# Splitting a third product of each pair once more, coupled over neighbouring couples, with two operands streamed from HBM

## What is computed

```
h    = rmsnorm(x, norm_g)
proj = einsum('btd,dc->btc', h, w_in)            # 1088 x 2048 x 10240
xa, za, v, bg, cg, zb, ga, gb = split(proj)
ya   = pool_mixer(xa, ...) * silu(za)            # trailing means, small 256x256 maps
yb   = bg * depthwise_conv3(cg * v) * silu(zb)
merged = sigmoid(ga + b) * (ya @ w_proj_pool) + sigmoid(gb + b) * (yb @ w_proj_conv)
y    = rmsnorm(x + merged @ w_out, final_norm_g)
```

## Time and profile before

| | |
|---|---|
| median of 3 runs | 2416.88 us |
| span of the profiled execution, first to last instruction | 2415.0 us |
| outside the span (run less span) | about 1.9 us |
| TensorE (PE) busy | 2392.6 us, 99% |
| VectorE (DVE) busy | 1700.3 us, 70% |
| ScalarE (ACT) busy | 894.0 us, 37% |
| GpSimd (POOL) busy | 116.0 us, 5% |
| granted TensorE clock | 0.998 of full speed over the span |
| HBM read and written | 172 GB/s over the span |

### The profile page before, as it was taken

How to read it: one execution, slowest core, us unless ns; L and a number is a source line. 1 busy time by engine, 2 the same in 40 slices (tenths; PEclk the granted TensorE clock), 3 DMA queues, 4 the chain that set the end, 5 groups by cost and what they waited for, 6 DMA issues and landing times.

```text
span 2415.0 us, 42738 instructions
## 1 busy us (share of the span) xinstructions
PE 2392.6 (99%) x17842; PEld 2332.7 (97%) x17842; DVE 1700.3 (70%) x2329; ACT 894.0 (37%) x1316; POOL 116.0 (5%) x220
## 2 busy tenths in 40 slices
PE   8999999999999999999999999999999999999998
PEld 7999999999999999999999999999999999888886
DVE  6676666666666586777868777765755887877676
ACT  7333333333333343323322222233533533532535
POOL 3010000000000000000000000000000011100000
PEclk9999999999999999999999999999999999999999
DMA  7563333232323454434433343345645767898656
GB/s 268 198 205 110 107 106 111 99 118 90 127 90 127 163 188 151 150 136 151 150 132 113 136 138 135 107 154 208 227 168 171 275 241 278 296 343 306 243 178 227
DMA packets 196655, 418.06 MB, mean 173 GB/s; under 512 B 12617, under 2 KB 114045, under 8 KB 182448
## 3 DMA queue, kind: packets, MB, share of 16 engines
q1 hardware_dynamic: 170928, 284.85, 35.0%
q0 software_dynamic: 23744, 125.24, 13.7%
q10 hardware_dynamic: 1792, 5.24, 0.6%
HBM read 281.00 MB, written 133.77 MB: 172 GB/s over the span
## 4 chain that ended last, share of the span: by engine, by line
PE 97%; DVE 0%; issue 0%; ACT 0%; DVEq 0%; POOL 0%; POOLq 0%; ACTq 0%
PE ps L1328 76%; PE ps L1475 12%; PE ps L1390 7%; PE ps L1497 1%; PE ps L1543 1%; DVE ops L2195 0%; ACT ops L1683 0%; DVE out L2458 0%; PE ps L1520 0%; DVE out L2511 0%; DVEq L226 0%; DVE h0raw L2612 0%; POOL rstd L1309 0%; ACT squares L1804 0%; ACT squares L1813 0%
## 5 line engine op out<-in xcount | busy, mean ns | idle before, releaser
L1328 PE MATMUL ps<-ops,hi 128*128 128x272 f32 x9728 | 1325.2, 288 | 0.1
L1328 PEld LDWEIGHTS ps<-ops,hi 128*128 128x128 f32 x9728 | 1264.5, 188 | 0.4 <-DVE ops L2195 0.3
L1328 PE MATMUL ps<-ops,lo 128*128 128x272 f32 x4864 | 708.6, 288 | 0.0
L1328 PEld LDWEIGHTS ps<-ops,lo 128*128 128x128 f32 x4864 | 647.4, 188 | 0.0
L1604 ACT ACTIVATE hi<-sb 128x512 fp32r<-128x512 f32 x440 | 278.2, 632 | 576.3 <-PE ps L1328 444.1
L2169 DVE TENSOR_TENSOR pb<-pb,ps 128x544 f32<-128x544 f32 x330 | 237.5, 720 | 261.8 <-PE ps L1328 261.6
L2025 DVE TENSOR_TENSOR lo<-sb,hi 128x512 fp32r<-128x512 f32 x440 | 303.1, 689 | 153.3 <-ACT hi L1604 148.7
L1604 ACT ACTIVATE hi<-raw 128x512 fp32r<-128x512 f32 x264 | 166.8, 632 | 371.6 <-PE ps L1328 357.6
L2025 DVE TENSOR_TENSOR lo<-raw,hi 128x512 fp32r<-128x512 f32 x264 | 181.8, 689 | 103.0 <-ACT hi L1604 103.0
L1475 PE MATMUL ps<-ms_hi,mt 128*128 128x512 f32 x896 | 221.3, 389 | 0.0
L1475 PEld LDWEIGHTS ps<-ms_hi,mt 128*128 128x128 f32 x896 | 168.2, 188 | 34.8
(11 more groups left out here) (173 smaller groups left out, 1580.2 us busy)
## 6 DMA issues: line engine op xcount, KB each, us to landing
raw<-in_w_in_dram SPq DMA_DIRECT2D x156, 512.0 KB, 4.0
pb<-part SPq DMA_DIRECT2D x39, 1088.0 KB, 6.0
part<-pb POOLq DMA_DIRECT2D x37, 1088.0 KB, 5.3
mt_raw<-opq SPq DMA_DIRECT2D x28, 1024.0 KB, 6.3
gates<-pb POOLq DMA_DIRECT2D x16, 1088.0 KB, 8.7
gate<-gates SPq DMA_DIRECT2D x32, 544.0 KB, 6.2
ms<-in_w_out_dram SPq DMA_DIRECT2D x16, 1024.0 KB, 9.5
ops_raw<-opq SPq DMA_DIRECT2D x15, 1088.0 KB, 6.8
```

What stands on the lines that cost most here:

```text
L1328: mm = nc.tensor.matmul(ps[b][:, c, 0:HC], w[:, w_slot, kt * P:(kt + 1) * P], operand[:, kt, half, c * HC:(c + 1) * HC], start=fresh and k ...
```

## The change

In 14 of the 16 turns (`LINKS`, a = 10, 12, ..., 36) product 3 is treated as 5 and 6 were: product 3 of pair a and product 3 of the pair before it, a - 1, which belongs to the turn before, become seven small products Q0 to Q6 of 6 MATMULs each. So product 3 of a pair b is finished one turn later; turn 8 leaves it out (`FIRST_LINK_TURN`) and the last turn computes that of pair 37 whole (`LAST_LINK_TURN`). Q products use one bank of `ps2` each instead of two.

To make room in SBUF, the block sums of products 5 and 6 no longer stay there: they are stored to HBM once (`kept_p`, 6 stores) and from turn 8 on each of L1, L2 and L4 loads its own (tile `ta`, 1088 KB a load, issued by SyncE when the one before has been used). The tiles they leave take the three block sums for product 3 (12 more `t2_step`s, in turn 8) and two kept weight sums (`s3`). The order of every turn from 8 on is new, as are the slots at which weight sums are made (`LATER_SUMS`), the slots of the loads, and who drains what: VectorE takes over (0, 2) from ScalarE in the linked turns and adds every Q product; (1, 1) is drained by VectorE, behind a copy that ScalarE makes elsewhere into the same tile.

The diff, cut to its core:

```diff
@@ -103,6 +103,15 @@
+    Q0, Q1, Q2, Q3, Q4, Q5, Q6 = range(2 * NQ, 3 * NQ)
+    LINK_TURN = ((0, 0), (0, L1), (0, 1), (0, L0), (0, 2), (0, Q0), (0, Q1), (0, L2), (0, 4), (0, L3), (0, Q2), (0, Q3),
+                 (1, 0), (0, Q4), (0, Q5), (0, L5), (1, 2), (0, L4), (0, Q6), (1, 1), (0, L6), (1, 4))
+    FIRST_LINK_TURN = ((0, 0), (0, L1), (0, 1), (0, L0), (0, 2), (0, 3), (0, L2), (0, 4), (0, L3), (1, 0), (0, L5),
+                       (1, 2), (0, L4), (1, 1), (0, L6), (1, 4))
+    LAST_LINK_TURN = (*LINK_TURN, (1, 3))
+    LINKS = QUADS[2:]
+    QUAD_TURNS = {a: QUAD_TURN if a == QUAD0 else FIRST_LINK_TURN if a == QUAD0 + 2 else
+                  LAST_LINK_TURN if a == QUADS[-1] else LINK_TURN for a in QUADS}
...
+    LATER_SUMS = {}
+    for a in QUADS[1:]:
+        s0 = BASE[a]
+        if a in LINKS:
+            LATER_SUMS |= {s0 + 4: [(a, 3)], s0 + 14: [(a + 1, 1)], s0 + 16: [(a + 1, 3)], s0 + 18: [(a + 1, 4)]}
+        else:
+            LATER_SUMS |= {s0 + 10: [(a + 1, 1)], s0 + 11: [(a + 1, 3)], s0 + 13: [(a + 1, 4)]}
...
+            by_act = q in (0, 1, L0, L1, L2, L6) or q == 2 and not (second and is_linked(g))
+            by_dve = q in (3, 4) or q >= NQ and q != L1 or \
+                q == 2 and second and is_linked(g) or not second and (q == 0 or q == 1 and is_linked(g))
         if by_dve:
             nd += 1
             dve_count[s] = nd
...
-        t2 = [[at(f"t2_{c}{i}", o, [2, 2, HC], F32R) for i, o in enumerate(T2_AT[c])] for c in (0, 1)]
-        t2_raw = [[at(f"t2_raw{c}{i}", o, [2, 2, HC]) for i, o in enumerate(T2_AT[c])] for c in (0, 1)]
+        t2 = [[at(f"t2_{c}{i}", o, [2, 2, HC], F32R) for i, o in enumerate(T2_AT[c % 2])] for c in (0, 1, 2)]
+        t2_raw = [[at(f"t2_raw{c}{i}", o, [2, 2, HC]) for i, o in enumerate(T2_AT[c % 2])] for c in (0, 1, 2)]
+        ta = at("ta", XE0, [2, 2, 2, HC], F32R)
+        s3 = at("s3", WS0 + DS_B, [2, KQ * P])
         raw_y = at("raw_y", DS0, [2 * KQ * P])
...
         STORED_AT[BASE[FIRST[YB]] + 2] = FIRST[YB] - 1
 
         QUAD_LOADS = {BASE[QUAD0 - 1] + 4: (2 * QUAD0 + 3,)}
         for a in QUADS:
-            last = a + 2 not in QUADS
-            for k, m in (((1, 2 * a + 2), (4, 2 * a + 5), (6, 2 * a + 4), (7, 2 * a + 7), (11, 2 * a + 6)) if last else
-                         ((1, 2 * a + 2), (6, 2 * a + 4), (9, 2 * a + 5), (11, 2 * a + 7))):
+            if a == QUAD0:
+                at_slots = ((1, 2 * a + 2), (6, 2 * a + 4), (9, 2 * a + 7), (11, 2 * a + 5))
+            elif a not in LINKS:
+                at_slots = ((4, 2 * a + 2), (9, 2 * a + 4), (10, 2 * a + 7), (12, 2 * a + 5))
+            elif a + 2 in QUADS:
+                at_slots = ((5, 2 * a + 2), (14, 2 * a + 4), (15, 2 * a + 7), (17, 2 * a + 5))
+            else:
+                at_slots = ((5, 2 * a + 2), (9, 2 * a + 5), (14, 2 * a + 4), (15, 2 * a + 6), (19, 2 * a + 7))
+            for k, m in at_slots:
...
             for k, o in enumerate(T2_OFF[c]):
                 T2_AT_SLOT.setdefault(t2_at + o, []).append((c, k))
+        for k, o in enumerate((1, 2, 3, 4, 5, 6, 7, 9, 12, 13, 14, 15)):
+            T2_AT_SLOT.setdefault(BASE[QUAD0 + 2] + o, []).append((2, k))
+
+        PIECE_STEPS = (L1, L2, L4)
+        PIECES = [(a, q) for a in QUADS[1:] for q in PIECE_STEPS]
+        PIECE_AT = {}
+        for a, q in PIECES:
+            if q == L1:
+                PIECE_AT[BASE[a - 2] + 13 if a == QUAD0 + 2 else SLOT[a - 2, L4] + 1] = (a, q)
+            else:
+                PIECE_AT[SLOT[a, PIECE_STEPS[PIECE_STEPS.index(q) - 1]] + 1] = (a, q)
 
...
+
+            def load_pieces(a, q):
+                n = PIECES.index((a, q))
+                if n == 0:
+                    sp.wait_ge(product_done, done_of(SLOT[QUAD0, L4]))
+                    sp.wait_ge(pieces_stored, 96)
+                else:
+                    sp.wait_ge(product_done, done_of(SLOT[PIECES[n - 1]]))
+                sp.dma_start(f32(ta[:, :, :, :, :]), kept_p[PIECE_STEPS.index(q)]).then_inc(ta_landed, 16)
...
-                    sp.wait_ge(b01_kept, 32)
+                    sp.wait_ge(b01_kept, 48)
                     sp.wait_ge(t2_kept, 32)
                     for c in (0, 1):
                         sp.dma_start(f32(b01(c)), kept_t[c]).then_inc(t4_landed, 16)
+                if s in PIECE_AT:
+                    load_pieces(*PIECE_AT[s])
+                if s == BASE[LINKS[0]] + 3:
+                    sp.wait_ge(product_done, done_of(SLOT[QUAD0 + 2, 3]))
+                    sp.wait_ge(t2_kept, 48)
+                    sp.dma_start(f32(b01(2)), kept_t[2]).then_inc(t4_third_landed, 16)
+                if s == SLOT[QUADS[-1], Q6] + 1:
+                    sp.wait_ge(product_done, done_of(SLOT[QUADS[-1], Q6]))
+                    sp.dma_start(f32(b01(2)), kept_b[2]).then_inc(b01_third_landed, 16)
...
-                    for c in (0, 1):
+                    for c in (0, 1, 2):
                         pool.dma_start(kept_b[c], f32(b01(c))).then_inc(b01_kept, 16)
                 for c in (0, 1):
+                    for i in range(3):
+                        if (c, 9 + i) in T2_AT_SLOT.get(s, ()):
+                            pool.wait_ge(t2_made[c], 10 + i)
+                            pool.dma_start(kept_p[i, :, c], f32(t2[c][i][:, :, :, :])).then_inc(pieces_stored, 16)
...
+                            t = t2[c] if a == QUAD0 else [ta[:, c, :, :, :]] * 3
+                            operand = (b_block(c, 0, 0), t[0], t[1], b_block(c, 1, 1), t[2],
                                        b_block(c, 1, 0), b01(c))[i]
...
+                    if w is lo:
+                        pe.wait_ge(w_lo, split_of_slot(s))
+                    elif half == 0:
+                        pe.wait_ge(w_hi, split_of_slot(s))
+                    for kt in range(2):
+                        mm = nc.tensor.matmul(psum(s), w[:, s % R, kt * P:(kt + 1) * P], operand[:, kt, half, :],
+                                              start=i in (0, 1, 5) and kt == 0 and w is hi and half == 0,
+                                              stop=kt == 1 and w is lo, skip_group_check=i not in (0, 1, 5))
+                mm.then_inc(product_done, 1)
+
             def product(s):
                 g, q = AT_SLOT[s]
...
 
+            def link_weight_sum(a, q):
+                dve.wait_ge(s_made, sums_of(a, {Q1: 3, Q2: Q1, Q3: Q2, Q4: 3}[q]))
+                if q == Q1:
+                    one, other, op = link_block(a, 0), link_block(a, 1), ALU.add
+                elif q == Q2:
+                    one, other, op = link_sum(a, Q1), link_block(a - 1, 0), ALU.subtract
+                elif q == Q3:
+                    one, other, op = link_block(a - 1, 1), link_sum(a, Q2), ALU.subtract
+                else:
+                    one, other, op = link_block(a - 1, 0), link_block(a, 0), ALU.subtract
...
+                    own, src = link_target(s), psum(s)
+                elif q in (L0, L2, L6):
+                    own, src = quad_target(s)[:, 0, :], psum(s)[:, 0, :]
+                elif q >= NQ:
+                    own, src = quad_target(s), psum(s)
+                elif (g, q) == (b, 0):
...
                     dve.wait_ge(pb_stored[ring(0)], stored_after[0])
+                if (c, k) == (2, 0):
+                    dve.wait_ge(product_done, done_of(SLOT[QUAD0, L4]))
```

More of the change, by code:

```diff
@@ L128, in first_of, with in_late_quad, is_linked @@
         return g - (g - QUAD0) % 2
+    def in_late_quad(g):
+        return in_quad(g) and first_of(g) > QUAD0
+    def is_linked(g):
+        return LINKS[0] - 1 <= g <= LINKS[-1]
     def pair_of(s):
@@ L462, in bass_hybrid_stream_step @@
         t_made = sem("t_made")
-        t2_made = [sem(f"t2_made{c}") for c in range(2)]
-        t2_hi = [sem(f"t2_hi{c}") for c in range(2)]
+        t2_made = [sem(f"t2_made{c}") for c in range(3)]
+        t2_hi = [sem(f"t2_hi{c}") for c in range(3)]
+        pieces_stored = sem("pieces_stored")
+        ta_landed = sem("ta_landed")
+        t4_third_landed = sem("t4_third_landed")
+        b01_third_landed = sem("b01_third_landed")
         t2_kept = sem("t2_kept")
@@ L1206, in whole_pair @@
                 if in_quad(g):
-                    for e in ((g, L2), (g, L5)) if g in QUADS else ((g, 2), (g, 4)):
+                    last = ((g, L2), (g, L5)) if g in QUADS else ((g, 2), (g, 4))
+                    if in_late_quad(g) and g in QUADS:
+                        last += ((g, Q6),) if g in LINKS else ()
+                    elif in_late_quad(g):
+                        last = (g - 1, L6), (g, 4), (g + 1, Q5) if is_linked(g) else (g, 3)
+                    for e in last:
                         wait_product_drained(pool, SLOT[e])
@@ L1371, in quad_product @@
                 i = q - NQ
-                if BANK_BEFORE[s] is not None:
-                    wait_product_drained(pe, BANK_BEFORE[s])
+                for before in BANK_BEFORE[s]:
+                    wait_product_drained(pe, before)
```

(11 more changed lines are left out.)

171 lines of the change are left out of this document (148 added, 23 removed).

## The result

| | median of the runs | lowest and highest | ratio to before, 95% interval |
|---|---|---|---|
| before | 2416.89 us (7 runs) | 2416.66 to 2417.83 | |
| after | 2422.99 us (7 runs) | 2420.90 to 2427.46 | 1.0029 (1.0019 to 1.0038) |

The profiled execution of after took 2426.41 us with a span of 2424.2, 3.4 above its median; 9.2 above the span of before. The runs of after also scatter over 6.6 us where before scatters over 1.2.

What follows compares the result with a forecast made beforehand. TensorE, 99% busy, bounds the kernel by MATMULs times their rate. Span 2415.0 - 10.6 + 1.5 + 0.3 + 0.3 = 2406.5, with 1.9 us outside it 2408.4 us, 0.35% faster; range 2406.0 to 2417.0.

Steps and rivals of the forecast that it cites:

- the streamed operands: `ta` loads for L1, L2 and L4 land in 6.0 to 6.8 us, in time; cost nothing, bounds 0 and 1.65 us a turn.
- The signs I had named for being wrong: A turn over 40.3 us, with a gap before L2 released by a DMA, or before L1 or (1, 0) behind a drain.
- MATMULs removed: In 14 linked turns TensorE runs 84 fewer MATMULs, all on the chain, at 0.1258 us each: 10.6 us saved.
- Weights in time: Weights made during the three slots before their use: spare for hi 1.6 us, lo about 3; halved but not gone.
- VectorE's load: VectorE rises to 31 of 39.95 us a linked turn, 78%, falling 1.2 to 1.5 us behind locally; cost nothing.
- Turn 8: TensorE waits before (1, 0) for VectorE's drain of (0, 4), VectorE being behind: 1.5 us once, bounds 0.2 and 4.
- the wait on the stored sums: In turn 8 one block sum waits until a 544 KB store has landed: 0.3 us once, bounds 0 and 3.
- Weight loads: Weight loads in the turns land in 5.3 us, VectorE waiting 0.3; cost nothing, bounds 0 and 0.5 us a turn.
- Last turn: Reload of the overwritten 544 KB token block before the whole (1, 3), covered by 7.5 us: 0.3 us, bounds 0 and 2.
- Rival C: L2's streamed load lands late every linked turn, `ta` having no second tile: slower, up to 2431.5 us; 9% with other slower ways.
- Rival B: VectorE becomes the bound locally in every linked turn, 0.5 us x 14 = 7 us: 2415.4 us, no change; 15%.
- Rival A: Everything hides, turn 8 and the last one costing under 0.5 us: 2406.3 to 2406.8 us; 14%.

## Why the prediction was wrong

The step that failed is the one on the streamed operands, "L4 to the next L1: 90, 11.3 us, less 0.6 behind a weight load ... At 6.8 the tightest has 2 us to spare. Cost nothing". The time available was nearly right: 10.7 us by the working, 10.35 measured. The landing was not: 10.2 to 11.8 us instead of 6.8. This step, put at nothing, cost 12.9 us of the profiled execution, of which the chain behind a late weight load has about 1 us of idling. I took the median of loads of that size, made a mean of the traffic (191 GB/s, measured 193), and asked which gap between products was shortest, L1 to L2. I did not ask what else is issued at the same moment. Every number for it stood ready: the change moves both stores of a turn behind Q5 and Q6, four slots apart, and I counted their drains but not their DMAs. The signs I had named for being wrong missed it too: the gap stands before L1, but behind a landing, where I had put a DMA only before L2 and only a drain before L1.

- **MATMULs removed**, 10.6 us: right, shown by the run with next to no load at L1.
- **Weights in time** and **VectorE's load**, nothing: right. 77% and no pause in that same run.
- **Turn 8**, 1.5 us with bounds 0.2 and 4: right place and releaser, 0.87 + 0.2 measured. Moving one block sum behind the drain took the pause to 0.24, so the mechanism is shown. The 0.3 us for the wait on the stored sums did not appear.
- **Weight loads**, bounds 0 and 0.5 us a turn: right for most turns, VectorE waited 0.5 to 1.4 us without a cost. Once it cost TensorE about 1 us of the pause of 2.42, through the drains of (1, 4) behind it, and with that perhaps the 1.6 of slower clock; the landing was 9.7 us, above the bound of 7.5.
- The Trainium skill's rule there ("DMA: Bandwidth & Descriptors", Issuing engines are not separate DMA queues), that all issuers share 16 engines and interleave, was weighed against the weight load of 512 KB only. The trace agrees with it at the seam, DMA share 0.84 to 1.01 for 12 us, and it should have been applied to the transfer issued last.
- **Last turn**, 0.3 us with bounds 0 and 2: the place was right, the size was 2.64 idle, 0.2 and 2.8 of slower clock. That is the second term that failed. The 10.1 us of landing lay above the 9.1 of the earlier trace rows, and 10.1 less the 7.5 of cover is the idle time; it alone is above the bound, and the clock stood in no term.
- **Rival C** had the mechanism, a late load and no second tile, but at L2, where loads landed in about 5.1 us. At L1 a landing costs already from 10.7 us by my working (10.35 measured), and the worst that I had, 10.5, stood just at it. I gave it 9% with other slow ways. **Rival B**'s drains of (1, 4) before L1 are the end of the pause at 416.60, once. **Rival A** was out with the first term that cost.
- One row was misread without effect: what I called two whole turns, 210 to 250.7 us, is one, of 40.70 us.

What stays open: why landings at the seam differ by 1.6 us from turn to turn and execution to execution. That the scatter of the runs goes with the load is shown (0.8 us with 32 KB of it, 6.6 in after, and 6.3 with the whole load and both ends mended); its source is not.

## What to carry to other kernels

Price a new transfer by what is issued within its own landing time, from all engines, and not by the mean traffic or the median landing of its size. When a reordering completes two results close together, their stores come close together too; list them beside the loads that the same slots release, each with its deadline. Then give the late user one more slot of cover (here (0, 1) ahead of L1) before touching the transfers themselves: each of these has a deadline of its own.

## What the runs showed that I had not expected

- A 32 KB load 0.4 us behind a 512 KB load in SyncE's queue landed with it, 6.0 us after its issue; a 512 KB load 0.4 us behind a 1088 KB one took 12.5 us. In both, the transfer ahead in the queue set the landing more than the transfer's own size; in three of thirteen seams the 32 KB came 1.0 to 2.5 us after the weights ahead of it, and why is open.
- A stop of TensorE cost about 0.2 us beyond its idle time, and the two of 2.42 and 2.64 us also 1.6 and 2.8 us at 1.2 GHz. Pauses of up to 1.52 us left the clock alone in every run; of two longer ones in other runs, it fell after one of 2.14 us and not after one of 2.26.
- Halving L1's load took its median landing only from 11.0 to 9.2 us, and 32 KB of it still took 5.9: about half of the landing is not its own bytes.
